# PEER stage of a hybrid decoder step: V rows gathered by token, one tile later, summed in four column groups

## What is computed

```python
q = (xt @ w_q).reshape(n, 8, 2, 128)
s1 = einsum('nhd,hkd->nhk', q[:, :, 0], keys1);  s2 = einsum('nhd,hkd->nhk', q[:, :, 1], keys2)
v1, i1 = top_k(s1, 16);  v2, i2 = top_k(s2, 16)
cand = v1[..., :, None] + v2[..., None, :];  cand_idx = i1[..., :, None] * 128 + i2[..., None, :]
top_s, sel = top_k(cand, 16);  idx = take_along_axis(cand_idx, sel);  g = softmax(top_s)
act = gelu(einsum('pd,ped->pe', xb, u[idx]))        # 128 rows of u per token
out = einsum('pe,ped->pd', g * act, v[idx])         # 128 rows of v per token
y = rmsnorm(h + out, norm_final)                    # h is the residual before the layer
```

## Time and profile before

| what | value |
|---|---|
| median of three executions | 4674.15 us |
| profiled execution, span | 4664.4 us |
| median less span | 9.75 us |
| stages before `peer_stage` end | about 1423 us into the span |
| first gather of the PEER stage | 1476.6 us |
| end of the last gather's issue | 4645.8 us |
| gathers | 2176 of 512 KB, 1088 for U and 1088 for V |
| busy over the span | PE 3850.8 us, DVE 2478.5 us, POOL 2471.3 us, ACT 1078.6 us |
| PE clock granted | mean 0.910 |

### The profile page before, as it was taken

The page is one execution under the profiler, slowest core; times in us unless marked ns, Lnnn a source line. Parts: engine busy times, 40 slices in busy tenths (PEclk is TensorE's granted clock), DMA queues, the critical chain, the costliest instruction groups (busy, mean ns, idle before and its releaser), DMA issues.

```text
span 4664.4 us, 46976 instructions
## 1 busy us (share of the span) xinstructions
PE 3850.8 (83%) x13480; PEld 2174.6 (47%) x13480; DVE 2478.5 (53%) x6136; ACT 1078.6 (23%) x2482; POOL 2471.3 (53%) x2212
## 2 busy tenths in 40 slices
PE   8999997899884878787887787787788787878787
PEld 7888885555442334343343343343334343434332
DVE  3111004655434666666666666666666666666665
ACT  4221113333210212212222212222222121212221
POOL 0000000000002777777777777777777777777766
PEclk9999997999967999898999898989898999898989
DMA  3222214221136999999999999999999999999988
GB/s 135 89 85 99 77 41 155 75 65 46 53 100 252 369 379 350 385 368 362 368 375 371 367 382 363 360 373 361 358 389 352 363 374 364 346 374 358 361 322 309
DMA packets 393667, 1291.38 MB, mean 277 GB/s; under 512 B 48440, under 2 KB 84536, under 8 KB 391368
## 3 DMA queue, kind: packets, MB, share of 16 engines
q0 software_dynamic: 313920, 1143.22, 65.1%
q1 hardware_dynamic: 61080, 116.93, 7.4%
q10 hardware_dynamic: 18432, 28.42, 1.7%
HBM read 1243.87 MB, written 45.71 MB: 276 GB/s over the span
## 4 chain that ended last, share of the span: by engine, by line
PE 30%; DVE 14%; DMA 12%; issue 8%; POOL 3%; ACT 2%; POOLq 0%; ACTq 0%; DVEq 0%; SPq 0%
PE e_o_ps L1776 24%; DMA e_u_rows<-in_u,e_expert 8%; PE e_q_ps L1744 4%; DMA e_v_rows<-in_v,e_expert 3%; POOL e_v_rows L1429 2%; POOL e_u_rows L1429 1%; DVE e_pairs L1583 1%; DVE e_pairs L1608 1%; DVE e_top_idx L1585 1%; DVE e_top_idx L1582 1%; DVE e_pairs L1612 1%; DVE e_picked L1614 1%; DVE e_top_val L1584 1%; DVE e_pos L1585 1%; PE e_w_ps L1731 1%
## 5 line engine op out<-in xcount | busy, mean ns | idle before, releaser
L1776 PE MATMUL e_o_ps<-e_v_rows,e_diag 128*128 128x512 f32 (+1 forms) x4352 | 2061.4, 626 | 380.7 <-ACT e_diag L1499 289.3
L1631 DVE CUSTOM_DVE_ANT_0 e_u_rows<-e_u_rows,e_xn 128x1024 f32<-128x1024 f32 x1088 | 1300.6, 1223 | 1058.0 <-DMA e_u_rows<-in_u,e_expert 974.5
L1776 PEld LDWEIGHTS e_o_ps<-e_v_rows,e_diag 128*128 128x128 f32 (+1 forms) x4352 | 828.9, 197 | 1464.2 <-issue 1375.3
L1429 POOL DMA_INDIRECT e_v_rows<-in_v,e_expert x1024 | 1177.2, 1150 | 351.1 <-issue 250.8
L1429 POOL DMA_INDIRECT e_u_rows<-in_u,e_expert x1024 | 1114.3, 1088 | 376.4 <-issue 268.7
L1499 ACT ACTIVATE e_diag<-e_ident,e_weight 128x128 f32<-128x128 f32 x1024 | 361.9, 395 | 872.9 <-PE e_o_ps L1776 869.4
L1744 PEld LDWEIGHTS e_q_ps<-e_xnT,e_wq 128*128 128x128 f32 x2304 | 307.7, 209 | 117.9 <-issue 109.2
L1744 PE MATMUL e_q_ps<-e_xnT,e_wq 128*128 128x128 f32 x2304 | 314.4, 294 | 40.3 <-issue 34.0
L578 POOL TENSOR_TENSOR p_gate<-p_gate,gn 128x1024 f32<-128x1024 f32 x8 | 18.9, 2357 | 448.9 <-DMA p_gate<-z_tok 448.9
L373 PE MATMUL j_m<-j_wh,j_xh 128*128 128x512 f32 (+1 forms) x648 | 248.0, 383 | 4.5 <-DVE j_wl L309 2.5
L374 PE MATMUL j_m<-j_wl,j_xh 128*128 128x512 f32 (+1 forms) x648 | 246.2, 380 | 0.0
(11 more groups left out here) (255 smaller groups left out, 3930.1 us busy)
## 6 DMA issues: line engine op xcount, KB each, us to landing
j_w<-in_w_big SPq DMA_DIRECT2D x12, 2048.0 KB, 8.1
z_tok<-j_stage ACTq DMA_DIRECT2D x64, 256.0 KB, 2.0
e_u_rows<-in_u,e_expert POOLq DMA_INDIRECT x1024, 6.3
e_v_rows<-in_v,e_expert POOLq DMA_INDIRECT x1024, 6.3
z_feat<-j_stage ACTq DMA_DIRECT2D x32, 256.0 KB, 2.0
e_wq<-in_wq SPq DMA_DIRECT2D x2, 4096.0 KB, 24.0
e_room<-merged SPq DMA_DIRECT2D x9, 512.0 KB, 6.6
e_h_next<-in_x SPq DMA_DIRECT2D x9, 512.0 KB, 9.3
```

The lines of the kernel that those rows point to most:

```text
L1429: pool.indirect_dma_start(ring[:, k % size, :], None, table, bass.IndirectOffsetOnAxis(ap=index[:, h % IDX, k:k + 1], axis=0)).then_inc(go ...
L1631: dve.tensor_tensor_reduce(u_rows[:, k % U_RING, :], u_rows[:, k % U_RING, :], xn[:, :], 1.0, 0.0, ALU.mult, ALU.add, dots[:, h % 2, k:k + ...
L1776: last = pe.matmul(o_ps[0:n, c * BANK:(c + 1) * BANK], diag[:, k % DIAGS, 0:n], v_rows[:, k % V_RING, c * BANK:(c + 1) * BANK], start=Fals ...
```

## The change

- V is gathered by token instead of by slot: one gather brings the 128 experts' rows of *one* token to the 128 partitions. For that, all expert numbers of a tile are kept as floats (`expert_f`), PE transposes them (`turn_experts`, once per tile, after the last quad of its last head), and DVE copies them back to whole numbers (`expert_T`). POOL waits for that copy (`iT_ready`) ahead of the first U gather of the next tile.
- V runs one tile later than U. Tile 0 has U gathers alone, the tiles 1 to 7 have 16 U and 16 V gathers per unit, `LAST` has 8 U and 16 V per unit, and then come 64 V gathers alone.
- Within a unit POOL issues four U, then four V, and so on (in `LAST` four U, eight V). The ring of U has 7 buffers instead of 8.
- Gelu and weights are made once per tile. The weights are transposed by PE (`turn_weights`). Instead of diagonals ACT writes one column of weights per token into a zeroed strip of 64 columns (`place`, four tokens in one instruction, two strips in turn); PE reads 32 columns of the strip, shifted so that the weights stand in the token's column.
- Four tokens (32 apart) are a *quad*: PE sums each one into its own 32 partitions of `o_ps`, with 128x32 weights, the four column groups in turn within each half of 512 columns. There are 32 quads a tile; a V buffer comes free when its quad is done.
- The residual isn't carried through PE; it is stored to DRAM (`keep_h`), loaded again (`load_h`) and added by DVE (`out_sum`). ACT squares it, and the final norm follows as before.
- `xn` has two buffers, so the copy `take` (L1576) goes. `select` loses its wait for `v_used` and a small copy, and gains a small copy of the expert numbers.
- All loops are written out (no `Fori`), and no waits stand in extra instructions (`wait_alone`). A block in which SP clears all semaphores of the first two stages one by one stands ahead of `peer_stage`, so that they can be used again.

The core of the diff:

```diff
-    U_RING, V_RING = 8, 8
+    U_RING, V_RING = 7, 8
...
-            def tile(t):
                 for h in range(HEADS):
-                    early = 0
...
-                    for k in range(TOPK):
-                        if k < slots(t):
-                            u_gather(t, h, k)
-                        if early + k < slots(t, h - 1) and not (isinstance(t, int) and t == 0 and h == 0):
-                            v_gather(t, h - 1, early + k)
+                    pool.wait_ge(picked_ready, t * HEADS + h + 1)
+                    if t and h == 0:
+                        pool.wait_ge(iT_ready, t)
+                    for k in range(0, slots(t), 4):
+                        for i in range(4):
+                            u_gather(t, h, k + i)
+                        if t:
+                            per = 4 * TOPK // slots(t)
+                            for n in range(per):
+                                v_gather(t - 1, h * TOPK + per * k // 4 + n)
+            pool.wait_ge(iT_ready, LAST + 1)
+            for n in range(NSAMP):
+                v_gather(LAST, n)
...
+            def v_gather(t, n):
+                j, g = divmod(n, lanes(t))
+                i = v_at(t, j, g)
+                wait(pool, v_used, quad_of(i - V_RING) + 1)
+                token = 32 * g + j
+                pool.indirect_dma_start(v_rows[:, i % V_RING, :], None, v_dram,
+                                        bass.IndirectOffsetOnAxis(ap=expert_T[:, t % 2, token:token + 1], axis=0)
+                                        ).then_inc(v_got[i % V_RING], 16)
...
+            def place(t, j):
+                q = t * QUADS + j
+                wait(act, v_used, q - 1)
+                n = lanes(t)
+                act.activation(window[:, q % 2, 0:n, 31], weight_T[:, j:j + 32 * (n - 1) + 1:32], ACT.Copy
+                               ).then_inc(window_ready, 1)
...
+                    for k in range(slots(t)):
+                        dot(t, h, k)
+                        if h == 0 and k == 2 and t:
+                            weights(t - 1)
+                        if h == 0 and k == 4 and t >= 2:
+                            out_sum(t - 2)
+                        if h == 0 and k == 6 and t >= 2:
+                            out_mean(t - 2)
+                        if h == 1 and k == 0 and t >= 2:
+                            out_norm(t - 2)
+                    if unit + 2 < UNITS:
+                        select(unit + 2)
+                    gates(unit)
+                    if h == HEADS - 1:
+                        turn_experts(t)
...
+            def quad(t, j):
+                n, q = lanes(t), t * QUADS + j
+                pe.wait_ge(window_ready, q + 1)
+                if j == 0:
+                    wait(pe, summed, t)
+                for g in range(n):
+                    i = v_at(t, j, g)
+                    pe.wait_ge(v_got[i % V_RING], 16 * (i // V_RING + 1))
                 for c in range(D // BANK):
+                    for g in range(n):
+                        last = pe.matmul(o_ps[32 * g:32 * g + 32, c * BANK:(c + 1) * BANK],
+                                         window[:, q % 2, g, 31 - j:63 - j],
+                                         v_rows[:, v_at(t, j, g) % V_RING, c * BANK:(c + 1) * BANK],
+                                         start=(j == 0), stop=(j == QUADS - 1))
+                last.then_inc(v_used, 1)
...
+        def reset():
+
+            with nc.Block() as block:
+                @block.sync
+                def _(sp):
+                    for used in named.values():
+                        sp.sem_clear(used)
+            free.extend(named.values())
+            named.clear()
```

More of the change, by code:

```diff
@@ L1516, in out_root @@
                 act.activation(stat[0:rows(t), 6:7], stat[0:rows(t), 5:6], ACT.Sqrt).then_inc(out_rt, 1)
-            act.wait_ge(made, 3)
+            act.wait_ge(made, 4)
             norm(0)
+            transposed(0)
             queries(0)
             queries(1)
-            exponentials(0, 0)
-            exponentials(1, 1)
-            def tile(t):
-                first = isinstance(t, int) and t == 0
-                last = isinstance(t, int) and t == LAST
+            exponentials(0)
@@ L1528, in tile @@
+            exponentials(1)
+            for t in range(LAST + 1):
                 for h in range(HEADS):
                     unit = t * HEADS + h
-                    if h == 1 and not first:
-                        out_root(t - 1)
-                    if h == HEADS - 2 and not last:
-                        norm(t + 1)
-                    if not (first and h == 0):
-                        diagonals(t, h - 1)
-                    if h < HEADS - 2 or not last:
-                        queries(unit + 2)
@@ L1538, in tile @@
-                    gelu(t, h)
-                    if h < HEADS - 2 or not last:
-                        exponentials(unit + 2, (h + 2) % HEADS)
-                    if h == 0 and not first:
-                        evacuate(t - 1)
-            tile(0)
-            with act.Fori(1, LAST) as t:
-                tile(t)
-            tile(LAST)
-            diagonals(LAST, HEADS - 1)
-            evacuate(LAST)
+                    if t and h == 0:
+                        gelu(t - 1)
+                        weights_turned(t - 1)
+                        place(t - 1, 0)
+                        place(t - 1, 1)
@@ new lines, in _ @@
+                    if t >= 2 and h == 0:
+                        out_square(t - 2)
+                        out_root(t - 2)
+                    if h == HEADS - 2 and t < LAST:
+                        norm(t + 1)
+                        transposed(t + 1)
+                    for part in range(4):
+                        j = 4 * h + part + 2
+                        if t and j < QUADS:
+                            place(t - 1, j)
+                        if part == 1 and unit + 2 < UNITS:
+                            queries(unit + 2)
@@ L1550, in _ @@
+                    if unit + 2 < UNITS:
+                        exponentials(unit + 2)
+            gelu(LAST)
+            weights_turned(LAST)
+            place(LAST, 0)
+            place(LAST, 1)
+            out_square(LAST - 1)
+            out_root(LAST - 1)
+            for j in range(2, QUADS):
+                place(LAST, j)
+            out_square(LAST)
             out_root(LAST)
@@ L1625, in u_dots @@
[L1625 to L1636 removed]
+                at = slice(h * TOPK, (h + 1) * TOPK)
@@ L1653, in out_mean, with turn_experts, out_sum @@
+            def turn_experts(t):
+                dve.wait_ge(iT_ps, t + 1)
+                dve.tensor_copy(expert_T[:, t % 2, :], t_ps[0].rearrange("p a n -> p (a n)")[:, 0:P]).then_inc(iT_ready, 1)
+            def out_sum(t):
+                n = rows(t)
+                dve.wait_ge(v_used, (t + 1) * QUADS)
+                dve.wait_ge(h_back, 16 * (t + 1))
+                dve.tensor_tensor(room[0:n, :], room[0:n, :], o_ps[0:n, :], ALU.add).then_inc(summed, 1)
             def out_mean(t):
@@ L1782, in _ @@
+            pe.wait_ge(made, 4)
             for part in range(4):
```

402 lines of the change are left out of this document (191 added, 211 removed).

## The result

The changed kernel takes 4706.62 us, median of four executions (4702.16 to 4718.99); the kernel before, beside it on the same chip, took 4670.18 us (4659.91 to 4674.29). The ratio is 1.0099, with a 95% interval of 1.0071 to 1.0127: the change makes the kernel about 1% slower. Forecast were 4655 us, 0.4% faster. The sign is wrong; the time lies in the range given.

The account below looks back on a forecast made before the run. POOL, issuing the gathers, was taken as the bound, not DMA. Terms 1771.1 + 2428 + 85 + 255 + 8.6 + 82 + 16 = 4645.7 us span; with the median 9.75 above, 4655 us, range 4570 to 4790.

Parts of the forecast that it names:

- first gather: POOL's first gather at 1484.0 us: 1476.6 plus 8 for clearing semaphores, less 0.6 for the dropped copy of `xn`.
- tile 0 with its stop: Tile 0, U alone, is bound by DVE: 8 x 34 = 272 us, plus 5.5 for residual and `norm`.
- chained dots: Tiles 1 to 7: only 4 dots run back to back behind each `select`, costing POOL 4 x 0.416 = 1.66 us.
- waits, head 6 and 0: Tiles 1 to 7: head 6, where `norm` delays dots and the U ring stops POOL, +4 us; head 0, -1.2.
- stops at the tile's end: POOL waits for `iT_ready` before the next tile's U gathers: 12.2 us, seven times 85 us; bounds 5.4 and 15.
- `LAST` with its stop: Last tile: 192 gathers x 1.25 = 240, extra 15, so 255 us; then 8.6 us for its own `iT_ready`.
- the price of a four: Four dots at landing pace, three times a unit, cost POOL 0.33 + 0.12 = 0.45 us; bounds 0 and 4 x 0.416.
- a random meeting: A POOL gather meeting a dot at a random phase waits at most 1.15, on average 0.57 us.
- the factor of 0.58: Single dots before cost POOL 0.305 us where random phases give 0.52; this ratio was applied to a four's first dot.
- B: Rival, chance 0.22: dots cost POOL what they did before, 5.5 us a unit; slower, 4806 us.
- A: Rival, chance 0.17: the lock costs the fours nothing and landings set the pace, 41.6 us a unit; 4577 us.
- C: Rival, chance 0.21: PE's column groups don't run side by side, a quad takes 7.03 us, not 1.76; 4676 us.

Follow-up runs that it names:

- experiment 1: The kernel before with only POOL's order changed, to four U then four V instead of one and one: 4501.33 us, ratio 0.965.
- experiment 9: The kernel before with only POOL's gathers put in runs of two U and two V: 4609.79 us, ratio 0.9888.
- experiment 3: The changed kernel with gathers alternating one U, one V (one U, two V in the last tile) instead of fours: 4833.36 us, ratio 1.037.
- experiment 2: The changed kernel with expert numbers transposed and copied back during head 7, POOL's wait moved to the first V gather: 4609.37 us, ratio 0.9893.
- experiment 4: The changed kernel with each dot over 64 of 1024 columns, sums left incomplete, all gathers and waits kept: 4523.32 us, one execution.

## Why the prediction was wrong

Its ledger of POOL against the trace, all in us of the profiled execution (the excess of the seven tiles is 210.8 us, parted between chained and other dots as in the table):

| step | forecast | measured | difference |
|---|---|---|---|
| first gather | 1484.0 | 1491.6 | +7.6 |
| tile 0 with its stop | 287.1 | 286.3 | -0.8 |
| tiles 1 to 7: 1792 gathers at 1.25 | 2240 | 2240 | 0 |
| chained dots | 93 | 96 | +3 |
| dots in fours | 76 | 115 | +39 |
| waits, head 6 and 0 | 20 | 36 | +16 |
| stops at the tile's end | 85 | 82 | -3 |
| `LAST` with its stop | 263.6 | 269.7 | +6 |
| 64 V alone | 82 | 84.9 | +3 |
| tail | 16 | 15.4 | -0.6 |
| sum (span) | 4645.7 | 4716.9 | +71 |

*The step that failed is the price of a four,* and in it the term for the three dots behind the first. The forecast took 0.33 us for the first dot (a random meeting of 0.57 us times 0.58, because single dots of the kernel before cost less than a random meeting should) and 0.12 for the other three, 0.45 in all. Measured are 0.70 us by the table, 0.66 in fours without a chained dot. In those the first dot costs 0.34 us, as forecast, and in the other orders 0.27 to 0.35: the factor of 0.58 carries over from single dots to fours. The other three cost 0.32 us and not 0.12. For three in order, landing 1.28 us apart, the working was right (0.03 us each). It left out that 70 of 396 come later than that and then cost 0.44 us, more than a first dot. The same is seen in the kernel before: 0.41 us in experiment 1, 0.22 for the one follower of a pair in experiment 9. That 0.57 + 0.12 makes 0.69 is a coincidence.

Why a first dot costs less than a random meeting can be read from the distances. In the kernel before, the next gather starts 1.0 to 1.25 us behind the dot's start, too late to lose much, for 47% of the 434 single dots of tiles 2 to 7; spread evenly over a period of 1.25 us it would be 20%. What sets that distance was not tested.

Here is a four of tile 2, in which the first dot meets a gather, the next two slip through, and the last comes 2.36 us behind the third:

```profile
2315.20 1.22 DVE L1644 CUSTOM_DVE_ANT_0 e_u_rows<-e_u_rows,e_xn 128x1024 f32<-128x1024 f32 x1 [5.84 <-DMA e_u_rows<-in_u,e_expert]
...
2315.47 1.77 POOL L1451 DMA_INDIRECT e_v_rows<-in_v,e_expert_T  x1 [0.30 <-issue]
...
2316.45 1.23 DVE L1644 CUSTOM_DVE_ANT_0 e_u_rows<-e_u_rows,e_xn 128x1024 f32<-128x1024 f32 x1
...
2317.55 0.95 POOL L1451 DMA_INDIRECT e_v_rows<-in_v,e_expert_T  x1 [0.30 <-PE e_o_ps L1799]
...
2317.74 1.23 DVE L1644 CUSTOM_DVE_ANT_0 e_u_rows<-e_u_rows,e_xn 128x1024 f32<-128x1024 f32 x1
...
2318.80 0.98 POOL L1451 DMA_INDIRECT e_v_rows<-in_v,e_expert_T  x1 [0.30 <-issue]
...
2320.10 1.25 DVE L1644 CUSTOM_DVE_ANT_0 e_u_rows<-e_u_rows,e_xn 128x1024 f32<-128x1024 f32 x1 [1.13 <-DMA e_u_rows<-in_u,e_expert]
```

A gather that starts 0.27 us behind a dot takes 1.77 us. With the dots 1.25 and 1.29 us apart, the next two start 0.13 and 0.17 us before a dot ends and take 0.95 and 0.98 us: they too end 0.82 us behind that dot's end, but had next to nothing to wait for. The Trainium skill's "SBUF — State Buffer", section "Who interferes with whom", says that a DVE instruction with two inputs in SBUF contends with a POOL instruction that reads SBUF, and calls the shared ports an exclusive lock. The 1.77 us agree: the first dot ends at 2316.42 and the gather at 2317.24, 0.82 us behind it.

*Waits at head 6.* The forecast had the U ring of seven stop POOL for some 2.5 us where `norm` delays the dots. The stop is there, once a tile at the 12th gather of head 6, and is 4.68 us in six of the seven tiles (2058.3, 2424.4, 2792.9 and so on); the right place, half the size. A few stops of 0.5 to 1.8 us elsewhere weren't foreseen. Experiment 1, with a ring of eight, has no wait above 0.5 us in tiles 0 to 7.

*The start.* In its own terms the forecast was near. SP's last store to the next stage's first load shows the clears:

```profile
1427.83 1.35 SPq L1073 DMA_DIRECT2D merged<-n_mT  x2
1438.62 0.63 SPq L1392 DMA_DIRECT2D e_wo<-in_wo  x1
```

and in the kernel before

```profile
1419.19 1.34 SPq L1073 DMA_DIRECT2D merged<-n_mT  x2
1423.75 0.61 SPq L1383 DMA_DIRECT2D e_wo<-in_wo  x1
```

10.8 against 4.6 us, so the clears cost 6.2 us where 8 were taken. The rest of the 15 us is the 8.6 us by which this execution reached that store later, in stages that the change doesn't touch.

*What was right.* The length of the stop at the tile's end (12.2 us forecast, 11.1 to 12.4 measured; 16.4 for the first, inside tile 0's sum), with `select` ending last ahead of the copy. Its lower bound was not: "5.4 if `select` weren't ahead of it" forgets the quad and the transpose of its own sentence, which give 8.6, and the trace has the transpose 1.3 to 2.5 us ahead of the copy. Tile 0, to 0.8 us. The chained dots: 4.3 a unit where 4 were forecast, 0.39 us each where 0.416 were taken (by this table's count the kernel before has 0.39 too). The forecast's reading of the first dot, as above. That V buffers of the steady tiles don't hold POOL up, that PE isn't on the path within the tiles, and that gathers set the pace at 1.25 us plus the lock.

*LAST.* The 6 us in the ledger are the stop of 8.1 us at its 17th gather, which the forecast didn't have, less some excess.

*From span to median.* The forecast took the span of before for one 9.75 us below the median. Time and span of one execution lie 2.1 us apart (4718.99 and 4716.9), so the profiled execution of before was some 8 us below its median. The span of the profiled one of after is 10.3 us above the median of 4706.6. The two together take 20 us off the 71, and leave the 52 us by which the forecast missed.

*The rivals.* B, slower since dots cost POOL what they did before, had the right sign but not its price: a unit lost 3.7 us to dots (1.70 + 2.04), not 5.5. It named the point from which it decides as 43.3 us a unit; measured are 43.7 plus 0.6 of waits. A, a lock that costs the fours nothing, is out by the table. C is out: the four products of a half start within 0.05 us of each other. A quad takes 3.64 us, twice the forecast 1.76, because PE's clock is at the lower of its two levels there (granted 0.50 over the quad at 2138.70; quads at 1.00 take 1.92), and within the tiles it hides nonetheless. Where the forecast went wrong as a judgement is the margin: a gain of 2.5 us a unit stood against 194 us of certain losses, with a bound of 1.66 against 0.45 us on the very term that decided.

Where the gain went, then: the fours are worth 127 us to this kernel (experiment 3), and the rest of the change costs more than that. Beside experiment 2, which is rid of the stops, the kernel of experiment 1 is 108 us faster (medians), most of it the loss of 88 us in tile 0 (265.6 us for 128 gathers, where its steady tiles need 177).

## What to carry to other kernels

Where POOL issues the gathers and DVE works on the rows, what POOL loses goes by how often a gather meets a dot, so group the gathers that feed DVE: runs of four nearly halved the price per dot and freed the other ring as well, for 3.5% in one changed loop. Runs of eight gained nothing over fours, and on a ring of seven they lost.

A price is read for each member of a group. Here the price of the first dot carried over from one order to the other; that the dots behind it were nearly free was read from a single row, and it holds only for rows that land on time. If the sign of the forecast hangs on such a term, cost it by its upper bound too, and say so.

And where a new wait is put at the head of a queue, look at all that its releaser stands behind, on every engine: here both `select` on DVE and the last quad on PE stood in front of one small copy, and moving the copy and the transpose ahead of both was worth 2%.

## What the runs showed of the hardware that was not expected

- Gathers of 512 KB land 1.28 us apart (410 GB/s) and average 1.30 us over a tile without its stop (experiment 4; 409 GB/s over 320 us), though DMA's share already read 0.96 at 1.456 us a gather.
- A dot over 64 columns takes 0.23 us and costs the gathers next to nothing: 10 us over 2176 of them.
- Products of 128x32 weights into four different groups of 32 output partitions run side by side in float32 whether they are issued group by group or half by half: 919.7 and 911.2 us busy, where the 4352 records last 0.95 us each.
- With PE less busy, its granted clock in the PEER stage fell from 0.90 to 0.68 (0.93 in experiment 1, where PE does the work of the kernel before in less time). Quads take 1.92 us at the full clock and mostly 3.64 in this kernel, at little cost to it.
- Dots landing less than 1.33 us apart cost the gathers 0.03 to 0.05 us each behind the first of their four, those that come later 0.44 (the changed kernel and experiment 1).
- The sequence of clears on SP costs 6.2 us by difference, about 0.06 us for each of the 100 semaphores counted.
